# Two attention stages of a decoder kernel: block sums on GpSimd, scores three tiles ahead, key weights in a copy

## What is computed

```python
# differential attention: q and k are normed over 64 columns, then times a weight
dq = rms_norm(dq.reshape(b, s, DIFF_HEADS, 2, DIFF_QK_DIM), q_norm_w)
dk = rms_norm(dk.reshape(b, s, DIFF_HEADS, 2, DIFF_QK_DIM), k_norm_w)
logits = einsum('bqhcd,bkhcd->bhcqk', qb, k) * scale + bias
p = softmax(where(mask, logits, -inf))
attn = p[:, :, 0] - lam * p[:, :, 1]
out = einsum('bhqk,bkhd->bqhd', attn, v)

# stick attention
z = einsum('bqhd,bkhd->bhqk', qb, k) * scale
log_1mb = where(mask, log_sigmoid(-z), 0.0)               # minus softplus(z)
rem = cumsum(log_1mb, axis=3, reverse=True) - log_1mb     # over the keys behind this one
a = where(mask, exp(log_sigmoid(z) + rem), 0.0)
out = einsum('bhqk,bkhd->bqhd', a, v)
```

## Time and profile before

| | us |
|---|---|
| median of three runs | 2120.02 (2119.59 to 2122.49) |
| the profiled execution | 2122.15 |
| its span | 2120.1 |

### The profile page before, as it was taken

The page is one execution under the profiler, slowest core; times in us unless marked ns, Lnnn a source line. Parts: engine busy times, 40 slices in busy tenths (PEclk is TensorE's granted clock), DMA queues, the critical chain, the costliest instruction groups (busy, mean ns, idle before and its releaser), DMA issues.

```text
span 2120.1 us, 42290 instructions
## 1 busy us (share of the span) xinstructions
PE 2083.4 (98%) x17622; PEld 1273.5 (60%) x17622; DVE 860.0 (41%) x1468; ACT 456.4 (22%) x740; POOL 356.2 (17%) x389
## 2 busy tenths in 40 slices
PE   9999999999999999999999999999999999999999
PEld 6888876354344354345343333347776778888887
DVE  4454435332333332333333332323565443544444
ACT  4152432000000000000000000023444523212221
POOL 2010001122222222322222222231201200000000
PEclk9999999999999999999999999999999999999999
DMA  7333114999999999999999999973111021332231
GB/s 259 99 120 129 65 35 189 413 405 406 406 405 408 405 405 410 402 403 408 399 403 405 402 407 395 401 276 113 60 60 40 1 80 60 99 99 99 79 100 59
DMA packets 157491, 520.01 MB, mean 245 GB/s; under 512 B 16460, under 2 KB 71936, under 8 KB 124576
## 3 DMA queue, kind: packets, MB, share of 16 engines
q1 hardware_dynamic: 136768, 495.02, 59.6%
q0 software_dynamic: 20672, 24.26, 4.9%
HBM read 509.09 MB, written 18.88 MB: 249 GB/s over the span
## 4 chain that ended last, share of the span: by engine, by line
PE 63%; DMA 11%; SPq 3%; DVE 2%; ACT 1%; POOL 1%; issue 1%; POOLq 0%; ACTq 0%; DVEq 0%
PE ps L2150 22%; PE ps L2164 12%; DMA ring_a<-in_w_down 8%; PE ps L395 8%; PE ps L397 8%; PE ps L396 8%; DMA ring_a<-in_w_gate_up 3%; SPq L576 2%; PE ps L1990 2%; SPq L574 1%; PE ps L2000 1%; POOL rstd L469 1%; PE ps L1982 1%; PE ps L497 0%; PE ps L2047 0%
## 5 line engine op out<-in xcount | busy, mean ns | idle before, releaser
L2150 PE MATMUL ps<-ring_a,xe 128*32 128x512 f32 x3912 | 433.6, 592 | 2.5 <-DMA ring_a<-in_w_gate_up 2.4
L2164 PE MATMUL ps<-ring_a,act_t 128*32 128x256 f32 x6000 | 335.0, 379 | 4.8 <-DMA ring_a<-in_w_down 3.3
L2150 PEld LDWEIGHTS ps<-ring_a,xe 128*32 128x32 f32 x3912 | 127.1, 110 | 282.3 <-issue 246.6
L2164 PEld LDWEIGHTS ps<-ring_a,act_t 128*32 128x32 f32 x6000 | 204.6, 110 | 142.8 <-issue 21.1
L2150 PE MATMUL ps<-ring_b,xe 128*32 128x512 f32 x2232 | 252.2, 593 | 0.0
L395 PE MATMUL ps<-xt_hi,hi 128*128 128x512 f32 x544 | 214.3, 394 | 0.8 <-DVE ff_a L1700 0.8
L396 PE MATMUL ps<-xt_lo,hi 128*128 128x512 f32 x544 | 212.3, 390 | 0.0
L397 PE MATMUL ps<-xt_hi,lo 128*128 128x512 f32 x544 | 212.3, 390 | 0.0
L1110 ACT ACTIVATE glu<-glu 128x768 f32<-128x768 f32 x32 | 27.0, 844 | 662.8 <-DVE glu L1653 662.8
L2150 PEld LDWEIGHTS ps<-ring_b,xe 128*32 128x32 f32 x2232 | 75.4, 110 | 142.9 <-issue 131.7
L767 POOL DMA_INDIRECT x_rows<-ye,idx x96 | 152.6, 1590 | 38.0 <-issue 38.0
(11 more groups left out here) (319 smaller groups left out, 2556.3 us busy)
## 6 DMA issues: line engine op xcount, KB each, us to landing
ring_a<-in_w_gate_up SPq DMA_DIRECT2D x163, 1024.0 KB
ring_a<-in_w_down SPq DMA_DIRECT2D x125, 1024.0 KB
ring_b<-in_w_gate_up SPq DMA_DIRECT2D x93, 1024.0 KB
raw<-in_w_in SPq DMA_DIRECT2D x20, 1024.0 KB, 6.6
raw<-in_w_gate SPq DMA_DIRECT2D x11, 1024.0 KB, 5.3
raw<-in_w_up SPq DMA_DIRECT2D x11, 1024.0 KB, 5.4
raw<-in_w_down SPq DMA_DIRECT2D x11, 1024.0 KB, 4.8
raw<-in_w_out SPq DMA_DIRECT2D x8, 1024.0 KB, 5.0
```

Source lines behind the costliest of these rows:

```text
L2150: last = pe.matmul(ps[QUAD * j:QUAD * j + QUAD, g, :], xe[:, g, QUAD * k:QUAD * k + QUAD], w[:, j, :, :, :], start=k == 0, stop=k == KT - 1)
L2164: last = pe.matmul(y_block(g, j, bank), act_t[:, g, QUAD * (2 * c + h):QUAD * (2 * c + h) + QUAD], w[:, h, QF * j:QF * j + QF], start=c == ...
```

## The change

There are three parts. (1) In `stick_cumulate` the six products with the square of -1 become five, four of them one block wide and one two blocks wide. POOL adds blocks of `sp` beforehand where several key tiles end in the same block of z (`sp_sum`, three additions of 128 columns for each head), and the last two products wait for these sums. (2) In the differential attention PE computes scores three steps ahead, DVE and ACT do logits and exponentials two steps ahead, and the first projection group is done before the first transpose of `att`. (3) `wqk` becomes one column (a number for each partition), and ACT multiplies by it when it copies `dkT` out of PSUM; DVE's second pass over k is gone.

```diff
--- before.py
+++ after.py
@@ -49,7 +49,7 @@
 C_EYE = C_QUAD + 1
 C_ALL = C_EYE + MAXB + 1
 
-S_CONV, S_GC, S_GF, S_ALL = 0, 12, 16, 20
+S_CONV, S_GC, S_GF, S_QN, S_KN, S_ALL = 0, 12, 16, 20, 21, 22
 R_L, R_QN, R_KN, R_DO, R_SB, R_BR, R_ALL = 0, 256, 320, 384, 512, 576, 608
 
 
@@ -240,9 +240,10 @@
         rel_w = at("rel_w", 136 * KB + 4 * SPAN, [32, DH])
         z_e = at("z_e", HT, [P, 2, T, SEQ])
         sp = at("sp", HT + 16 * KB, [P, 2, T, SEQ])
+        sp_sum = at("sp_sum", 120 * KB, [P, 2, 3, P])
         a_sb = at("a_sb", K(40), [P, 2, T, SEQ])
         sq_h = at("sq_h", K(56), [P, 2, T * 64])
-        wqk = at("wqk", K(56) + 256, [P, 64])
+        wqk = at("wqk", K(56) + 256, [P, 1])
         sqj = at("sqj", K(40), [P, 2, T, CONV])
         lam_p = at("lam_p", K(42.5), [P, 64])
         ff_a = at("ff_a", K(0), [P, 2, SEQ])
@@ -721,6 +722,12 @@
                 sh = sp[:, h % 2, :, 0:P]
                 pool.affine_select(out=sh, in_=sh, compare_op=ALU.is_gt, fill=0.0, base=0,
                                    pattern=[[0, T], [1, P]], channel_multiplier=-1).then_inc(s_spm, 1)
+                block = lambda j, b: sp[:, h % 2, j, b * P:(b + 1) * P]
+                pool.wait_ge(s_spm, 4 * h + 1)
+                pool.tensor_tensor(sp_sum[:, h % 2, 0, :], block(2, 1), block(3, 0), ALU.add).then_inc(s_spm, 1)
+                pool.tensor_tensor(sp_sum[:, h % 2, 1, :], block(1, 1), block(2, 0), ALU.add).then_inc(s_spm, 1)
+                pool.wait_ge(s_spm, 4 * h + 3)
+                pool.tensor_tensor(sp_sum[:, h % 2, 2, :], block(1, 2), sp_sum[:, h % 2, 0, :], ALU.add).then_inc(s_spm, 1)
 
             def head_rstd(i, o, n, w):
 
@@ -970,7 +977,10 @@
                     act.activation(sqj[:, :, :, :], dqk[:, :, :, :], ACT.Square).then_inc(hn_sq, 1)
             for i in range(2 * DH):
                 act.wait_ge(qk_t, i + 1)
-                copy((dqT, dkT)[i // DH][:, i % DH, :], ps[:, 4 + i % 4, :]).then_inc(qk_te, 1)
+                if i < DH:
+                    copy(dqT[:, i, :], ps[:, 4 + i % 4, :]).then_inc(qk_te, 1)
+                else:
+                    act.activation(dkT[:, i - DH, :], ps[:, 4 + i % 4, :], ACT.Copy, scale=wqk[:, 0:1]).then_inc(qk_te, 1)
 
             def diff_exp(n):
                 h, q = divmod(n, T)
@@ -988,8 +998,8 @@
                 if n >= 2:
                     act.wait_ge(d_o, n - 1)
                 copy(attT[:, n % 2, 0:q + 1, :], ps[:, 4, 0:(q + 1) * P]).then_inc(d_te, 1)
-                if n + 1 < DH * T:
-                    diff_exp(n + 1)
+                if n + 2 < DH * T:
+                    diff_exp(n + 2)
                 g = SB.first[B_SQ] + n
                 if g == SB.first[chunk_of(SB, g)]:
                     hi_part(act, SB, chunk_of(SB, g) + 2)
@@ -1013,6 +1023,7 @@
 
             act.preload_act_table_set("natural_log_exp_and_others")
             diff_exp(0)
+            diff_exp(1)
             for n in range(DH * T):
                 diff_evac(n)
 
@@ -1356,16 +1367,13 @@
                         dve.wait_ge(rel_flip, h + 1)
                         link(dve.tensor_copy(relT[:, h, :], ps[:, 4 + h, :]))
                     link(dve.memset(relT[0:64, :, SEQ - 64:SEQ], MASKED))
-            link(dve.scalar_tensor_tensor(wqk[:, :], rows[:, R_QN:R_QN + 64], 64 ** -0.5, rows[:, R_KN:R_KN + 64],
+            link(dve.scalar_tensor_tensor(wqk[:, :], scal[:, S_QN:S_QN + 1], 64 ** -0.5, scal[:, S_KN:S_KN + 1],
                                           ALU.mult, ALU.mult))
             for i in range(2):
                 dve.wait_ge(hn_rstd, i + 1)
                 v = dqk[:, i, :, :].rearrange("p t (g d) -> p (t g) d", d=64)
-                scaled = dve.tensor_tensor(v, v, rstd[:, 32 * i:32 * i + 32].unsqueeze(2).to_broadcast([P, 32, 64]),
-                                           ALU.mult)
-                link(scaled) if i else scaled.then_inc(qk_n, 1)
-            v = dqk[:, 1, :, :].rearrange("p t (g d) -> p (t g) d", d=64)
-            dve.tensor_tensor(v, v, wqk[:, :].unsqueeze(1).to_broadcast([P, 32, 64]), ALU.mult).then_inc(qk_n, 1)
+                dve.tensor_tensor(v, v, rstd[:, 32 * i:32 * i + 32].unsqueeze(2).to_broadcast([P, 32, 64]),
+                                  ALU.mult).then_inc(qk_n, 1)
 
             def diff_logits(n):
                 h, q = divmod(n, T)
@@ -1401,10 +1409,11 @@
                                   ALU.mult).then_inc(y_n, 1)
 
             diff_logits(0)
+            diff_logits(1)
             for n in range(DH * T):
                 diff_attn(n)
-                if n + 1 < DH * T:
-                    diff_logits(n + 1)
+                if n + 2 < DH * T:
+                    diff_logits(n + 2)
 
                 g = SB.first[B_SQ] + n - 1
                 if n and g == SB.first[chunk_of(SB, g)]:
@@ -1944,11 +1953,21 @@
                               dkT[o:o + 64, h, 0:(q + 1) * P], start=True, stop=True)
                 last.then_inc(d_s, 1)
 
-            diff_score(0)
+            def project(g):
+                c = chunk_of(SB, g)
+                pe.wait_ge(SB.lo_ready, c + 1)
+                if B_SV <= c < B_SK:
+                    group_tokens(pe, SB, c, g, xt_hi, xt_lo)
+                else:
+                    group_features(pe, SB, c, g, xt_hi, xt_lo, SEQ)
+
+            for n in range(3):
+                diff_score(n)
+            project(SB.first[B_SQ])
             for n in range(DH * T):
                 h, q = divmod(n, T)
-                if n + 1 < DH * T:
-                    diff_score(n + 1)
+                if n + 3 < DH * T:
+                    diff_score(n + 3)
                 pe.wait_ge(d_a, n + 1)
                 if n:
                     pe.wait_ge(d_te, n)
@@ -1956,13 +1975,8 @@
                     last = pe.transpose(ps[:, 4, k * P:(k + 1) * P], att[:, n % 2, k * P:(k + 1) * P], ident)
                 last.then_inc(d_t, 1)
 
-                g = SB.first[B_SQ] + n
-                c = chunk_of(SB, g)
-                pe.wait_ge(SB.lo_ready, c + 1)
-                if B_SV <= c < B_SK:
-                    group_tokens(pe, SB, c, g, xt_hi, xt_lo)
-                else:
-                    group_features(pe, SB, c, g, xt_hi, xt_lo, SEQ)
+                if n:
+                    project(SB.first[B_SQ] + n)
                 pe.wait_ge(d_te, n + 1)
                 if n:
                     pe.wait_ge(d_oe, n)
@@ -1984,12 +1998,20 @@
 
             def stick_cumulate(h):
 
-                pe.wait_ge(s_spm, h + 1)
+                def add(j, b, w, what):
+                    return mm(stick_z(h, j)[:, b * P:(b + w) * P], cc(w_col), what, start=False, stop=True,
+                              skip_group_check=True)
+
+                pe.wait_ge(s_spm, 4 * h + 1)
+                w_col = C_NTRI
                 for j in range(T):
-                    for m in range(j, T):
-                        last = mm(stick_z(h, j)[:, (m - j) * P:], cc(C_NTRI if m == j else C_NONES),
-                                  sp[:, h % 2, m, 0:SEQ - m * P], start=False, stop=True, skip_group_check=True)
-                last.then_inc(s_c, 1)
+                    add(j, 0, T - j, sp[:, h % 2, j, 0:SEQ - j * P])
+                w_col = C_NONES
+                for j in range(T - 1):
+                    add(j, 1, 1, sp[:, h % 2, j + 1, 0:P])
+                pe.wait_ge(s_spm, 4 * h + 4)
+                add(1, 2, 1, sp_sum[:, h % 2, 0, :])
+                add(0, 2, 2, sp_sum[:, h % 2, 1:3, :]).then_inc(s_c, 1)
 
             def stick_values(h):
                 pe.wait_ge(s_am, h + 1)
@@ -2264,7 +2286,8 @@
 
     conv = np.asarray(inputs["conv_w"]).reshape(3, 4, P).transpose(2, 0, 1).reshape(P, 12)
     gc, gf = (flat(n).reshape(4, P).T for n in ("g_conv_out", "g_fft_out"))
-    arrays["scal"] = np.ascontiguousarray(np.concatenate([conv, gc, gf], axis=1))
+    qn, kn = (np.tile(flat(n), 2)[:, None] for n in ("q_norm_w_2", "k_norm_w_2"))
+    arrays["scal"] = np.ascontiguousarray(np.concatenate([conv, gc, gf, qn, kn], axis=1))
     arrays["rows"] = np.concatenate([flat(n) for n in (
         "lambda_q1_2", "lambda_k1_2", "lambda_q2_2", "lambda_k2_2", "q_norm_w_2", "k_norm_w_2",
         "diff_out_norm_w_2", "sb_out_norm_w_2", "b_router")])[None, :]
```

## The result

The changed kernel took 2113.06 us, as the median of 9 executions (2111.20 to 2117.16). The ratio is 0.9946, with a 95% interval of 0.9936 to 0.9955: faster by 0.54%, about 11.5 us. The forecast was 12.6 us of gain and 2107.4 us. The size of the change came out nearly as forecast, but the time lies 0.06 us above the range's high end of 2113.0. These 0.06 us are well inside the spread of the executions, and the same kernel had a median of 2112.46 later.

A forecast was written before the change was run, and what follows sets the result against it. PE, busy nearly all of the span, was taken as the bound. Gains of 1.4 (weights of k), 2.7 and 4.0 (differential), 4.5 (stick) sum to 12.6 us: 2120.0 to 2107.4 us, range 2103.8 to 2113.

The forecast's parts named there:

- The anchor: Whole execution: the gain is subtracted from 2120.0 us, the median of the runs of the kernel before.
- Weights of k: Transposes of k: DVE's second pass goes, 1.8 us, and ACT's weighted copies cost 0.4; gain 1.4 us (1.1 to 1.8).
- Differential stage: Start gains 2.7 us from the first `att` wait and lower clock; four later `att` waits gain 4.0 (0 to 4.0).
- The two small waits: Start of differential attention: PE newly waits 0.5 us for DVE to read scores and 0.7 us for ACT's copy.
- Stick attention: Heads 2 to 6 gain 4.45 us, head 7 0.89 less 0.3, head 1 loses 0.5: 4.5 us (4.0 to 6.0).
- that of head 0: Stick attention's head 0: cumulation ends sooner, but PE's 1.2 us wait for ACT grows by 0.9, so nothing is gained.
- rival (a): The clock falls elsewhere, at the differential start or behind head 0; once costs 1.4 us, twice 2.8: about 2109.5; chance 0.15.
- The step for head 1: Stick attention's head 1: POOL's additions cost DVE's scaling 1.2 us, ACT comes late, head 3's logits wait: 0.5 us lost.
- (b): Stick attention: POOL's sums come late, or exponential and masks bound a head; stick gain gone, 2111.9 us; chance 0.10.
- (d): Stick attention: additions cost so much that each head's cumulation waits; slower from 2.2 us each, 2132 at 2.8; chance 0.04.
- Rival (c): Differential attention: DVE's queue stays the bound, so the four later `att` waits remain; 2111.4 us; chance 0.08.
- (e): Both attentions: the stick gain is gone and the later `att` waits remain; 2115.9 us, within 0.2%; chance 0.06.

The follow-up runs named there:

- before again: The kernel before the change, unaltered, run again as a control: 2124.41 us, ratio 1.0003.
- warm head 0: The changed kernel plus four products without use where PE waits for ACT's exponentials in head 0 of stick attention: 2111.41 us, ratio 0.9932 to the kernel before.
- projection in place: The changed kernel with the first projection group back between the first transpose of `att` and its product: 2111.08 us, ratio 0.9937 to the kernel before.
- sums alone: The kernel before with only POOL's block additions and the shorter cumulation added: 2121.35 us, ratio 0.9984 to the kernel before.
- after again: The changed kernel, unaltered, run again: 2112.46 us, ratio 0.9940 to the kernel before.
- additions x 4: The changed kernel plus nine further POOL additions per head, into a tile nobody reads, ahead of the three: 2126.34 us, ratio 1.0009 to the kernel before.
- scale spread: The changed kernel with DVE's scaling spread over heads 1 to 4, without head 1's three products without use: 2111.84 us, ratio 0.9945 to the kernel before.
- ahead alone: The kernel before with only scores three ahead, logits and exponentials two ahead, and the earlier projection: 2117.23 us, ratio 0.9964 to the kernel before.

## Why the prediction was right in its size and wrong in its time

1. **The anchor failed.** The step "from the median, 2120.0 - 12.6 = 2107.4" took the median of three executions for that of the kernel. 34 later ones had 2124.63, 4.6 us more, and the batches after them 2124.54 to 2126.69. Where the three low ones gained their time is not known; the two traces of before differ ahead of the attentions only (before again). The allowance of 0.4 to 1 us for the spread of runs, which also made the high end of the range, was too small; against 2124.6 the sum of 12.6 gives 2112.0. That the sum itself came within 1.0 us of the measured 11.59 is in part luck, as the differential stage gained 0.7 more and stick attention 1.7 less than forecast.
2. **Weights of k**: 1.4 forecast, 1.34 measured. The copies cost 0.4 more, as forecast. The wait for `dkT` is 1.51 us rather than 1.2.
3. **Differential stage**: 2.7 + 4.0 = 6.7 forecast, 7.43 measured. All five waits for `att` are gone, 6.6 us, and so is the fall of the clock. The forecast priced it at 1.4 from windows that end at 1520; windows of before from 1517 to 1519 and from 1519 to 1521 read 0.53 and 0.61, which makes 1.7, an estimate, and it cost 1.6 in the trace where it came back (warm head 0). The two small waits cost 0.55 + 0.37 instead of 0.5 + 0.7. 6.6 + 1.7 - 0.9 = 7.4. What was wrong is the reason given for the start: it is the depth that covers `att` of step 0, and the projection need not stand ahead of the transpose (projection in place).
4. **Stick attention**: 4.5 forecast, 2.82 measured. Heads 2 to 7: from the logits of head 3 to t, before took 1700.74 - 1641.69 = 59.05 us and after 1691.73 - 1637.76 = 53.97, a gain of 5.08, where 4.45 + 0.89 - 0.3 = 5.04 was forecast. Heads 0 and 1: from z to the logits of head 3 before took 1641.69 - 1616.57 = 25.12 us and after 1637.76 - 1610.38 = 27.38, a loss of 2.26, where 0.5 was forecast. 5.08 - 2.26 = 2.82. The step that failed here is that of head 0, "that wait grows by 0.9: nothing gained": it put the clock behind the longer wait at nothing. The wait did become 0.85 longer (2.04), and the clock fell behind it (after, sums alone, after again). This is rival (a) at head 0, named with a chance of 0.15 and a price of 1.4; it cost some 2.3 (warm head 0). The step for head 1, that DVE's stretched scaling makes ACT late and the logits of head 3 wait for it, had the size of the delay wrong, 0.64 us instead of 1.2: ACT's exponentials start 24.42 us after z instead of 1640.35 - 1616.57 = 23.78. No wait shows, as PE was later still behind the lower clock. With the clock up PE would have waited, and stick attention would have gained about 2.8 + 2.3 = 5.1 us (an estimate).
5. **The additions**: 0.48 us forecast for one, 0.45 measured, and never waited for. Rivals (b) and (d) are refuted, (d) also by what nine more additions did: the kernel came to 1.0009 of before. The Trainium skill's rule that such sums belong on VectorE ("GPSIMD Engine Reference", section "4.1 Engine selection") would have lost PE's time only past that cover; no run here put them on VectorE.
6. **DVE beside GpSimd**: forecast was 1.2 us lost by DVE in head 1; its eight scalings took 1631.19 - 1624.69 = 6.50 us in all instead of 1636.74 - 1630.88 = 5.86 in before (the earlier trace rows and the line below), 0.64 lost, and ACT came later by as much. Both engines were slowed, neither stood whole: an addition of 0.45 took up to 0.90. "SBUF — State Buffer", section "Who interferes with whom", in the Trainium skill calls the lock on the ports that the two share exclusive. If each stood for the whole of the other's instruction, DVE would have lost all of the three additions, some 1.4 us by estimate. The trace does not bear that out for this pair, and neither did that of before, which the prediction read as agreement: there too both were longer at once. The loss of 0.8 that it gave by that rule comes to 0.7 from its own rows (1640.35 + 1.4 + 0.6 - 1641.69).

```profile
1636.74 1.68 DVE L1416 TENSOR_SCALAR z_e<-ps 128x512 int32<-128x512 int32 x4
```

7. Rival (c) is refuted by the missing waits for `att`, and (e) with it.

Still open is what in head 0 sets off the fall. That the work ahead of the 2.0 us wait alone does it is unlikely: additions x 4 has waits of 2.11 us (head 0, with another 0.69 close behind) and 2.10 us (head 7) for the sums, and the clock fell behind both. But no run varied the length of the wait by itself.

## What to carry to other kernels

Cutting TensorE's work ahead of a wait makes the wait longer, and what follows can take back part of the gain: look at the granted clock behind each wait that grows, and fill the wait with products that outlast it as little as possible. Then look at what the engine would have waited for next at the full clock, since a fall can hide it. Where a stage waits because scores and exponentials run one step ahead, scores three ahead and exponentials two ended all the waits for `att` at once, and where the independent work stands among them mattered little. Forecast the stretch that the change touches, which repeats here to 0.03 us where the clock does not fall differently, and give the time of a whole execution the spread that three runs don't show, 10 us here.

## What the runs showed that was not expected

**A fall at one place comes with the program, at another with the execution.** In head 0 of the stick stage the clock held in all four traces with a wait of 1.2 us, fell in all five with 2.0 us (after, after again, sums alone, scale spread, projection in place), and held in all four with filler products. At the start of the differential stage it fell in the four traces where PE stood 2.6 us for `att`; of the ten with scores three tiles ahead, where that wait is gone, it fell in two (warm head 0 and additions x 4), though others with the same instructions up to there held. Additions x 4 is outside of the count for head 0, as it waits there for the sums first; its clock fell too. These are the windows of warm head 0 at that place; in after they read 1.00.

```profile
1514.80:1516.80 2.00, 1.45 (x6) 0.44 (x4) 1.90 (x5) 1.36 (x6) 0.00 (x0) 0.68 0.00 0
1516.80:1518.80 2.00, 2.00 (x6) 1.49 (x5) 1.78 (x5) 1.03 (x4) 0.00 (x0) 0.50 0.00 0
1518.80:1520.80 2.00, 2.00 (x10) 1.61 (x9) 1.89 (x5) 0.00 (x0) 0.00 (x0) 0.96 0.01 4
```

**Where executions differ.** From q to t, both kernels that were traced twice repeat to 0.03 us, and from t to the end all 14 traces agree to 0.2. Other kernels with the same code in a stretch differ there by 1.2 to 1.6 us where the clock fell for longer (sums alone) or fell at all (warm head 0), so this can come between executions as well. The first 1500 us spread over 6 us. In one trace (scale spread, q at 1511.13) PE waited 1.9 us there for a transfer of `gain`, which the earliest (ahead alone, q at 1505.18) does not show; the rest of the spread was not followed up.
